# Gaps of 64 bytes between the tiles that hold split matmul operands, in a two-layer decoder trunk on one core

## The reference, cut to what matters

```
for i in range(2):
    h = rms_norm(x, norm1_g[i])
    mix = even_mixer(h, ...) if i == 0 else odd_mixer(h, ...)
    x = x + mix
    h = rms_norm(x, norm2_g[i])
    x = x + square(relu(h @ mlp_w1[i])) @ mlp_w2[i]
```

## Time and profile before

| | |
|---|---|
| median of 3 runs | 1431.37 us (1431.27 to 1431.8) |
| the profiled execution | 1431.33 us, of which the span of instructions is 1429.6 us |
| PE busy | 1396.9 us, 98% of the span |
| DVE, ACT, POOL busy | 668.8, 599.9, 526.5 us |
| PE's share of the chain that ended last | 91% |
| granted clock of PE | 1.0 of full speed, whole span |

### The profile page before, as it was taken

One profiled execution on the slowest core, in us unless ns is written; L12 is line 12 of the kernel. 1 busy time (PEld: TensorE's weight loads), 2 busy tenths in 40 slices (PEclk: granted clock), 3 DMA queues, 4 the chain that ended last, 5 costly groups with the idle time before them and its releaser, 6 DMA issues.

```text
span 1429.6 us, 24988 instructions
## 1 busy us (share of the span) xinstructions
PE 1396.9 (98%) x10495; PEld 1147.7 (80%) x10495; DVE 668.8 (47%) x1112; ACT 599.9 (42%) x866; POOL 526.5 (37%) x239
## 2 busy tenths in 40 slices
PE   7999999999999999999999999999999999999998
PEld 5787778889878888888889977775688888888887
DVE  4665767788753314122144358936543223131231
ACT  5524763445545313232234465568635223131331
POOL 3544332111133543444345224332333443444341
PEclk9999999999999999999999999999999999999999
DMA  5332300000133233223224122210033223323221
GB/s 151 89 101 77 83 20 3 4 4 3 62 104 103 89 96 103 96 88 112 94 89 119 30 89 89 88 60 1 1 102 105 88 88 108 99 88 111 95 89 59
DMA packets 128977, 110.13 MB, mean 77 GB/s; under 512 B 10742, under 2 KB 126576, under 8 KB 128880
## 3 DMA queue, kind: packets, MB, share of 16 engines
q1 hardware_dynamic: 128000, 107.12, 24.1%
q10 hardware_dynamic: 880, 1.59, 0.3%
HBM read 106.60 MB, written 2.10 MB: 76 GB/s over the span
## 4 chain that ended last, share of the span: by engine, by line
PE 91%; DVE 3%; ACT 2%; POOL 2%; issue 1%; DMA 1%; SPq 0%; ACTq 0%; DVEq 0%; POOLq 0%
PE ps L570 23%; PE ps L571 23%; PE ps L575 23%; PE ps L707 5%; PE ps L1141 2%; PE ps L1151 1%; PE ps L1162 1%; PE ps L715 1%; PE ps L607 1%; PE ps L1116 1%; POOL pw_lo L2382 1%; PE ps L938 1%; PE ps L939 1%; PE ps L945 1%; PE ps L722 1%
## 5 line engine op out<-in xcount | busy, mean ns | idle before, releaser
L2469 POOL TENSOR_TENSOR w_lo<-lower,w_hi 128x2048 fp32r<-128x2048 f32 x83 | 385.6, 4645 | 523.6 <-ACT w_hi L1233 508.8
L570 PE MATMUL ps<-h_hi,w_hi 128*128 128x512 f32 x736 | 288.5, 392 | 1.2 <-ACT h_hi L1546 0.8
L571 PE MATMUL ps<-h_hi,w_lo 128*128 128x512 f32 x736 | 286.5, 389 | 0.0
L1233 ACT ACTIVATE w_hi<-lower 128x2048 fp32r<-128x2048 f32 x83 | 158.6, 1910 | 226.2 <-PE ps L575 226.2
L570 PE MATMUL ps<-a_hi,w_hi 128*128 128x512 f32 x480 | 186.7, 389 | 0.0
L571 PE MATMUL ps<-a_hi,w_lo 128*128 128x512 f32 x480 | 186.7, 389 | 0.0
L575 PE MATMUL ps<-h_lo,w_hi 128*128 128x512 f32 x736 | 181.8, 389 | 0.0
L570 PEld LDWEIGHTS ps<-h_hi,w_hi 128*128 128x128 f32 x736 | 138.1, 188 | 33.8 <-issue 4.3
L2174 DVE TENSOR_TENSOR lower<-lower,ps 128x512 f32<-128x512 f32 x60 | 41.3, 688 | 261.3 <-PE ps L575 261.3
L571 PEld LDWEIGHTS ps<-h_hi,w_lo 128*128 128x128 f32 x736 | 138.2, 188 | 29.2 <-issue 0.7
L575 PEld LDWEIGHTS ps<-h_lo,w_hi 128*128 128x128 f32 x736 | 138.1, 188 | 28.8
(11 more groups left out here) (410 smaller groups left out, 2032.0 us busy)
## 6 DMA issues: line engine op xcount, KB each, us to landing
lower<-in_mlp_w_dram SPq DMA_DIRECT2D x64, 1024.0 KB, 5.2
lower<-in_ev_w_in_dram SPq DMA_DIRECT2D x30, 512.0 KB, 3.9
lower<-in_od_w_in_dram SPq DMA_DIRECT2D x10, 1024.0 KB, 5.1
lower<-in_ev_w_out_dram SPq DMA_DIRECT2D x4, 1024.0 KB, 6.2
lower<-in_od_w_out_dram SPq DMA_DIRECT2D x4, 1024.0 KB, 4.9
lower<-in_od_w_in_dram SPq DMA_DIRECT2D x6, 256.0 KB, 3.9
out_dram<-lower SPq DMA_DIRECT2D x6, 256.0 KB, 2.5
upper<-in_x_dram SPq DMA_DIRECT2D x1, 1024.0 KB, 7.2
```

The costliest lines, as they stand in the source:

```text
L570: pe.matmul(o, wh, xh, start=(i_ == 0), stop=False)
L571: pe.matmul(o, wl, xh, start=False, stop=False)
L1233: act.activation(w_high(u)[:, :, 0:w], RAW[:, u % 2, :, 0:w], ACT.Copy).then_inc(hi_ready, 1)
L2469: pool.tensor_tensor(w_low(u)[:, :, 0:w], RAW[:, u % 2, :, 0:w], as_f32(w_high(u)[:, :, 0:w]), ALU.subtract)\
```

## The change

A constant STAGGER of 16 words (64 bytes) is added. An empty tile of that size is put below h_lo, one below w_hi and one below w_lo. So h_lo and h_hi lie 64 bytes higher than before, w_hi 128 bytes and w_lo 192 bytes; a_hi and a_lo stay, and so do the raw buffers and all tiles of the first layer's input projection. The offsets from which the recurrences' stores and `PT[1]` are computed are raised to match. No instruction is added, removed or moved.

```diff
-        ARENA, PARTS = 53000, 28224
+        ARENA, PARTS, STAGGER = 53000, 28224, 16
...
-        AH, AL, HL, HH = (parts(n_, 1, KT, W)[:, 0] for n_ in ("a_hi", "a_lo", "h_lo", "h_hi"))
-        WHB, WLB = (ctx.enter_context(nc.sbuf_tensor(n_, [P, 2, KT * USLOT], F32R)) for n_ in ("w_hi", "w_lo"))
+        AH, AL = (parts(n_, 1, KT, W)[:, 0] for n_ in ("a_hi", "a_lo"))
+        ctx.enter_context(nc.sbuf_tensor("below_h", [P, STAGGER], F32))
+        HL, HH = (parts(n_, 1, KT, W)[:, 0] for n_ in ("h_lo", "h_hi"))
+        ctx.enter_context(nc.sbuf_tensor("below_w_hi", [P, STAGGER], F32))
+        WHB = ctx.enter_context(nc.sbuf_tensor("w_hi", [P, 2, KT * USLOT], F32R))
+        ctx.enter_context(nc.sbuf_tensor("below_w_lo", [P, STAGGER], F32))
+        WLB = ctx.enter_context(nc.sbuf_tensor("w_lo", [P, 2, KT * USLOT], F32R))
...
-        o_whi = PARTS + 4 * KT * W
+        o_whi = PARTS + 4 * KT * W + 3 * STAGGER
...
-        o_wh1, o_wl1 = PARTS + 4 * KT * W, PARTS + 4 * KT * W + 2 * KT * USLOT
+        o_wh1 = PARTS + 4 * KT * W + 2 * STAGGER
+        o_wl1 = o_wh1 + 2 * KT * USLOT + STAGGER
```

## The result

The changed kernel takes 1447.62 us (median of 4 runs, 1446.11 to 1448.44), the kernel before 1431.32: a ratio of 1.0109, with a 95% interval of 1.0097 to 1.0121. It is slower by 16.3 us, where no change was forecast. The value lies at the upper end of rival B (1438.5 to 1447.9) and outside the stated range.

A forecast was written before the change was run, and what follows sets the result against it. PE's matmul count times the distance between starts was taken to bound the kernel. The profiled 1429.6 + 0 + 1.7 us around the span gave 1431.3, stated as 1431.4 us from the runs' median; range 1420 to 1442.

The forecast's parts named there:

- rival B: 512-column streams in the MLPs no longer settle because the relation alternates: 228.6 to 231.1 ns, 1438.5 to 1447.9 us; chance 0.19.
- What bounds the kernel: In both MLPs PE is busy 50.00 of 50 us; time is matmul count times the distance between starts.
- The matmuls that it touches: 3744 matmuls of 512 columns in L570, L571, L575, L996, L997, L1004: 848.6 us, 3.7 us per nanosecond.
- The step that failed: 512-column streams settle to whole 64-byte steps, so moving one operand against the other by 64 bytes costs 0 us.
- The reading of the earlier trace: 16-column weight loads at 228.6 ns, 1.9 ns longer, taken as strongest ground against a clash the gaps could cure.
- The bound: High bound for the 3744 matmuls if streams never settle: +1.9 to +4.4 ns each, +7.1 to +16.5 us.
- The unit with the uneven relation: Unit u_ikv, k stride 1056 bytes: 256 columns at 118.7 and 116.2 ns against 120.0, stream not settling.
- D: Rival: 512-column streams settle 1.3 to 3.8 ns lower, 4.9 to 14.2 us less, 1417.2 to 1426.5 us; chance 0.11.
- Case A: The forecast itself, no change in the matmul distance: 1431.4 us, 1429.5 to 1433.3; chance 0.63.
- The cover of ACT and POOL: Rounding into w_hi and subtraction into w_lo are hidden; they could grow by 4.3 us before PE waits.
- C: Rival: an address clash is real and goes, 512-column distance falls to about 215.3 ns, 1389 us; chance 0.07.
- The rule on ports: PE reads moving operand and weights through two ports and waits on no one, making the change worth exactly 0.

The follow-up runs named there:

- e_all64: Kernel before plus one 64-byte gap below a_hi, so a, h, w_hi, w_lo all move 64 bytes together: 1431.51 us, ratio 1.0001.
- m1_relations: Separate kernel of matmul streams alone, weights in steps of 32 bytes above the streamed tile: 226.67 ns at 0 and 256 bytes, 233.33 at 64.
- e_w64: Kernel before plus one 64-byte gap below w_hi, so w_hi and w_lo lie 64 bytes above a and h: 1455.3 us, ratio 1.0168.
- m4_short: Separate kernel of streams alone, with loads of 16 or 64 columns, or 256 streamed columns, at several relations: 16-column loads settle at 226.7 to 231.7 ns.
- m3_pairs: Separate kernel of streams alone, loads alternating between two weight tiles at paired relations: 226.7 ns at (0,0), 230.0 at (64,128), 232.5 at (0,64).

## Why the prediction was wrong, point by point

- **What bounds the kernel** was right: PE never waits in the MLPs, before or after, and the whole change of time is a change of the distance between starts.
- **The matmuls that it touches** was right: 3744 of 512 columns, 3.7 us for each nanosecond. 16.9 us of excess over 3744 are 4.5 ns. The 256-column ones, which the prediction left out as far fewer, moved the other way, by -1.5 us.
- **The step that failed** is "a stream that settles to whole steps of 64 bytes looks the same when everything is moved by 64 bytes, or one operand against the other by 64". Its first half holds (e_all64: ratio 1.0001). Its second half is false: 64 bytes of one against the other are 226.7 to 233.3 ns (m1_relations), and 1431.7 to 1455.3 us in the kernel (e_w64). That distances settle at multiples of 6.667 ns says something of time, and I read it as something of addresses. x, pw and a, h, w give one number because all have relation 0 and 256 is the period, not because 64 bytes don't matter.
- **The reading of the earlier trace rows** was the support of that step, and misled. I took the 228.6 ns with 16-column loads as proof that weight reads don't take the stream's slots at equal addresses. m4_short shows that such loads depend on the relation as well, 226.7 to 231.7 ns, and only have their best place elsewhere. One row at one relation could not tell.
- **The bound** held as a number, and in part by luck: 228.6 to 231.1 ns for a stream that does not settle, read from the earlier trace rows, gave 1438.5 to 1447.9, and the runs lie at 1447.6. But 226.7 + 4.5 = 231.2 ns is already past its end, h_lo at 233.4 is well past it, and e_w64, at 233.3 ns in the mean of its moved streams, took 1455.3 us; the -1.5 us of the 256 columns, which the bound left out, helps to keep the time inside. Its mechanism was right in kind (the tiles' relation takes the stream out of its settled state) but not in its condition: B blamed the alternation, while the constant relation of 64 bytes is worse (e_w64). The streams also do settle, only into slower cycles. The unit with the uneven relation in the earlier trace rows was the one place among the split products of that trace where relations other than 0 occurred. It said that the relation counts, which the prediction set aside; but its distances were shorter (116.2 and 118.7 against 120.0 ns), so for the direction it spoke for D and misled.
- **Range and chances.** Case A at 0.63 was too high for a value that no row showed; the range cut B in its middle.
- **The cover of ACT and POOL** held: POOL's w_lo waited longer for its work (539.2 us of idle time on the page, from 523.6), and PE's waits did not grow.
- **Rivals C and D** are refused for 512 columns at the constant relations tried: 226.7 ns is the least of 34 of the 64 places, and no uneven pair in m3_pairs is below 230.0. What D took from the earlier trace rows is true of 256 columns (113.3 in place of 120.0 ns for h with a) and did not carry over to 512. The Trainium skill's page "TensorE: Matmul & The Clock Gate", section "Back-to-back issue gap", gives 215.8 ns for 512 columns as the gap of isolated matmuls on a warm clock; no relation tried comes within 10 ns of it. The 13.3 ns between the 213.3 ns of 512 columns at 2.4 GHz and 226.7 ns stay unexplained.
- **The rule on ports.** The Trainium skill's page "SBUF — State Buffer", section "Who interferes with whom", has PE's two read ports wait on no one. The ratio of 1.0168 for e_w64 disagrees in so far as the place of the weights changes how fast PE streams. Whether the ports themselves collide, or the sequencing of load and stream in some other way, no run here tells.

**What the whole change is, by the runs' own numbers:** from the groups without other work, h pairs at 230.0 (+3.3 ns, 1472 matmuls, +4.9 us), h_lo at 233.3 (+6.7, 736, +4.9), a pairs at 230.0 (+3.3, 1024, +3.4), a_lo at 232.4 to 233.3 (+5.7 to 6.7, 512, +2.9 to 3.4), and -1.5 for 256 columns: +14.6 to 15.1 us, beside 14.8 in the span. The medians stand 16.3 apart; the profiled execution (1446.11 us) is the shortest of its four, and no trace of the others is there to say where they spend 1 to 2 us more.

## What to carry to other kernels

When PE is the bound, measure the distance between starts of successive matmuls, and look at where weights and streamed operand lie modulo 256 bytes: two tiles of fp32r that agree there ran at 226.7 ns a matmul of 512 columns, and all but two of the other 33 relations tried at 228.9 to 234.4, up to 1.7% of this kernel's time. Tiles of whole multiples of 256 bytes get this for nothing; a small tile or a pad put between them can take it away. And where a trace holds a single value of a quantity (here relation 0 for 512 columns), a rule by which other values are the same is a guess, however well the multiples fit. A row of another kind (here 256 columns with uneven relations) can tell that the quantity counts, and needs a run of its own before it tells how much or in which direction.

## What the runs showed of the hardware that was not expected

- The relation acts with a period of 256 bytes and a grain of 4: 248 bytes is as good as 0, 252 and 4 are 6.7 ns worse. What makes 0, 144 and 248 good stays open.
- Settled streams are cycles whose sum is a whole multiple of 6.667 ns: one matmul of 226.67 (34 steps), two of 233.33 (231 and 236, 70 steps together), three of 228.9 (229, 232, 226: 103 steps), two of 230.0 (69 steps). All 68 groups of the five kernels of streams end in such a cycle, of at most 24 matmuls. Of the 63 that started at the full clock 60 repeat it to within 2 ns from the seventh distance behind the wait at the latest; the others took 9, 14 and 25.
- For streams of 256 columns 0 bytes is not the best place: 116.8 against 119.8 ns in the changed kernel, with 113.3 for h with a; in m4_short 116.7 at 192 bytes against 118.3 at 0 (and 120.0 at 128). The same relation gives different values there and in the kernel (0 bytes: 118.3 and 120.0; 192 bytes: 116.7 and 113.3), and why was not tried. A kernel that gave the two kinds weights at different relations might gain 1.5 us here, 0.1%, an estimate from the changed kernel; that was not tried, and it is as small as the intervals of these runs. No version beat the kernel before.
